# Two opening weight units taken through the input tiles together, their weights loaded in halves

## The chip, the cores and the metric

The program runs on one core of one Trainium2 chip. The metric is the device time of one execution in microseconds (us), lower is better. Each kernel is executed several times, and the median is compared.

## The reference, cut to what matters

The program computes a dilated attention block, a retention block and a stick-breaking attention block, each followed by a gated feed-forward layer, on 512 positions of width 1024 in float32. The change touches only the first normalisation and the first products of the first block:

```python
def rms_norm(x, g):
    xf = x.astype(jnp.float32)
    y = xf * lax.rsqrt(jnp.mean(xf * xf, axis=-1, keepdims=True) + EPS)
    return (y * g.astype(jnp.float32)).astype(x.dtype)
...
    h = rms_norm(x, ln_pre_mix[l])
    proj = h @ w_in[l]
    u_pool = proj[..., :POOL_WIDTH]
    q = proj[..., POOL_WIDTH:POOL_WIDTH + ATTN_WIDTH].reshape(B, S, N_HEADS, HEAD_DIM)
    k = proj[..., POOL_WIDTH + ATTN_WIDTH:POOL_WIDTH + 2 * ATTN_WIDTH].reshape(B, S, N_HEADS, HEAD_DIM)
    v = proj[..., POOL_WIDTH + 2 * ATTN_WIDTH:].reshape(B, S, N_HEADS, HEAD_DIM)
    q, k = rope(q, pos), rope(k, pos)
```

The 256 columns of `u_pool` are two blocks of 128 columns; each of the six head pairs then takes one block of q, one of k and one of v.

## The kernel before

**Units.** The input lies transposed in eight tiles of 128x512 (`X[:, c, :]`, c = 0 to 7). All weights come as a stream of units: a unit is a block of 1024 rows by 128 columns, 512 KB, in eight 128x128 pieces. To reach float32 precision, every input tile and every unit is split into a high part and a low part in a shorter format: HH and HL of the input, WH and WL of the weights. A unit is 24 matmul passes of 128x512 on TensorE (PE): for each of eight pieces WH with HH, WH with HL, and WL with HH. Units 0 and 1 are the two pooling blocks, unit 2 the q block, unit 3 the k block and unit 4 the v block of the first head pair.

**Who does what.** ScalarE (ACT) makes HH (`input_hi`, L1527) and WH (`split_hi`, L375, and two half copies at L1830 and L1833). VectorE (DVE) makes HL (`input_lo`, L2182). GpSimd (POOL) makes WL by a subtraction of a whole unit, 128x1024 (`split_lo`, L647), except for unit 0, which DVE makes in two halves of 128x512 (L2603, L2608). There are two sets of RAW, WH and WL: even units use set 0 and odd units set 1; unit 4 has a raw buffer of its own, RAW7, but uses WH and WL of set 0. The load of a unit into a raw buffer waits until the low part of the unit two before it is made (semaphore `s_lo`), because that subtraction reads the raw buffer.

**The queues.** The SyncE queue (SP) issues in program order: the gains, x tiles 1 and 2, the second half of unit 0, x tiles 5 and 7, the first half of unit 1, then unit 2 (which waits for the low part of unit 0), then seven constant tables (L589), then unit 4 (L592), unit 3 and unit 5 (L570). The ACT queue issues x tile 0, the first half of unit 0, x tiles 3, 4 and 6, and the second half of unit 1.

**TensorE's order.** Three products of zeros (L1149), then `first_unit` for unit 0, which goes tile by tile with its low part two tiles behind (L1138, L1141, L1142); then unit 1 whole (`use_unit`: `high_part`, L394 and L395, then `low_part`, L403); then the first attention stage, `attn_stage(0, None)`: the high part of unit 2, the mean of the squares (`mean_of_sum`, L714), the low part of unit 2, unit 3 whole, and unit 4. Before unit 4 PE waits until DVE has turned the q block (`a_qk`), because unit 4 writes the same PSUM bank as unit 2.

**The norm.** The inverse root of the mean is not applied to the input but to the results. ACT squares the eight tiles (L1837), DVE adds them up into ACC (`add_squares`, L2501 and L2504), PE takes the mean over partitions (L714), ACT forms the logarithm into ACC (L1536) and the exponential into RB (L1538). DVE multiplies the cosine and sine tables by RB (L2617, CS1 and SN1), multiplies the q block by the cosine table (L2660), ACT copies the halves of the q block crosswise (L1875), and DVE multiplies by the sine table and adds (L2664, L2668), which gives QT1. POOL's subtraction for unit 1 waits until all HL are made, and that for unit 2 and the following ones until all squares are added.

```python
                    pool.wait_ge(s_h, DC)
                    split_lo(Unit(1), chunks)

                    pool.wait_ge(s_sq_used, DC)
                    for n in range(2, 6):
                        split_lo(Unit(n), chunks)
```

On ACT the order after the eight HH is: WH of unit 1, eight squares, WH of unit 2, WH of unit 3, MEANR (L1841, a copy of a constant), the logarithm, the exponential, WH of unit 4, the four crosswise copies.

Of the kernel before, what the change touches and what calls it, by code (L numbers as in the profile page):

```python
# [135 lines left out]
def build(nc, ins, out_t):  # L136
    ctx = ExitStack()
    with ctx:
# [423 lines left out]
        def _(sp):  # L562
# [11 lines left out]
            for count, chunks, large in STRETCHES:  # L574
                stream = ins["w_large" if large else "w_small"].rearrange("u p (c n) -> u p c n", c=chunks)
                start = 0
                if first == 0:
# [4 lines left out]
                    sp.dma_start(RAW[0][:, 4:DC, :], stream[0][:, 4:DC, :]).then_inc(s_raw[0], 16)  # L582
                    for c in (5, 7):
                        sp.dma_start(X[:, c, :], ins["x_t"][:, c, :]).then_inc(s_x_in[c], 16)
                    sp.dma_start(RAW[1][:, 0:4, :], stream[1][:, 0:4, :]).then_inc(s_raw[1], 16)
# [4 lines left out]

                    sp.wait_ge(s_raw[0], Unit(2).m * 16 + 16)
                    sp.dma_start(RAW7[:], stream[4]).then_inc(s_raw[0], 16)  # L592
                    load_unit(Unit(3), stream[3], chunks)
# [46 lines left out]
        def _(pool):  # L640
# [19 lines left out]
            for count, chunks in stretches:  # L660
# [5 lines left out]
                if first == 0:  # L666

                    pool.wait_ge(s_h, DC)
                    split_lo(Unit(1), chunks)

                    pool.wait_ge(s_sq_used, DC)
                    for n in range(2, 6):
                        split_lo(Unit(n), chunks)
                    start = 3
# [34 lines left out]
        def _(pe):  # L709
# [420 lines left out]
            def first_unit(u, bank):  # L1130

                for c in range(DC + 2):
                    if c in (0, 4):
                        pe.wait_ge(*((s_first_hi, 1) if c == 0 else (s_hi, u.index + 1)))
                    if c in (2, 6):
                        pe.wait_ge(*((s_first_lo, 1) if c == 2 else (s_lo, u.index + 1)))
                    if c >= 2:
                        mm = pe.matmul(bank, WL[u.s][:, c - 2, :], HH[:, c - 2, :], start=False, stop=(c == DC + 1))  # L1138
                    if c < DC:
                        pe.wait_ge(s_h, c + 1)  # L1140
                        pe.matmul(bank, WH[u.s][:, c, :], HH[:, c, :], start=(c == 0), stop=False)  # L1141
                        hi = pe.matmul(bank, WH[u.s][:, c, :], HL[:, c, :], start=False, stop=False)  # L1142
                        if c == DC - 1:
                            hi.then_inc(s_hi_used, 1)
                mm.then_inc(s_unit, 1)
# [4 lines left out]
            first_unit(Unit(0), B[2][:])  # L1150
            use_unit(pe, Unit(1), B[3][:], DC, HH, HL)
# [365 lines left out]
        def _(act):  # L1517
# [646 lines left out]
        def _(dve):  # L2164
# [331 lines left out]
            def add_squares(n):  # L2496

                for c in range(1, DC):
# [3 lines left out]
                    else:  # L2502
                        dve.wait_ge(s_sq_used, 8 * n + c)
                        dve.tensor_tensor(ACC[:], ACC[:], SQ4[:, c, :], ALU.add).then_inc(s_sq_used, 1)  # L2504

# [91 lines left out]
            for c in range(DC):  # L2597
                dve.wait_ge(s_x_in[c], 16)
                input_lo(0, c, G_MIX1)
                if c == 1:  # L2600
                    dve.wait_ge(s_first, 16)
                    dve.wait_ge(s_first_hi, 1)
                    dve.tensor_tensor(WL[0][:, 0:4, :], RAW[0][:, 0:4, :], WH[0][:, 0:4, :].bitcast(F32),  # L2603
                                      ALU.subtract).then_inc(s_first_lo, 1)
                if c == 3:
                    dve.wait_ge(s_raw[0], 16)
                    dve.wait_ge(s_hi, 1)
# [533 lines left out]
```

## Time and profile before

| | |
|---|---|
| median of 3 runs | 1918.2 us (1917.78 to 1918.5) |
| the profiled execution's own time | 1917.92 us |
| its span in the trace | 1916.0 us |
| PE busy | 1908.2 us |
| DVE, ACT, POOL busy | 1146.5, 880.0, 466.8 us |
| granted TensorE clock | 1.000 |
| read from HBM | 174.30 MB |

The profiled execution's own time is 1.9 us above its span, which is what lies around the first and the last instruction. Matmuls overlap, so a busy time per matmul is longer than the distance between two starts; distances are read from the starts.

### The profile page before, as it was taken

How to read it: one execution, taken by the hardware profiler on the slowest of the kernel's cores; microseconds unless marked ns; L12 is line 12 of the kernel's file. 1: busy time of each engine (PE TensorE's matmuls, PEld its weight loads, DVE VectorE, ACT ScalarE, POOL GpSimd, SP SyncE). 2: the span in 40 equal slices, each digit the busy share in tenths (PEclk: the TensorE clock that was granted, in tenths of full speed). 3: DMA queues.
4: the chain of work that ended last, by engine and by line, in shares of the span. 5: the costliest groups of instructions: out<-in, count | busy, mean ns of one | idle time of the engine just before them, and what ended most of it. 6: DMA issues, size and time to landing. Idle time of an engine off the chain costs nothing.

```text
span 1916.0 us, 28674 instructions
## 1 busy us (share of the span) xinstructions
PE 1908.2 (100%) x10163; PEld 1614.7 (84%) x10163; DVE 1146.5 (60%) x1663; ACT 880.0 (46%) x1370; POOL 466.8 (24%) x181
## 2 busy tenths in 40 slices
PE   9999999999999999999999999999999999999999
PEld 6777889998888888888889998888777788999887
DVE  5775688866237455464267787423777768877500
ACT  6665544435234434434254444324667554444421
POOL 3323300003423343343420000443322240000243
PEclk9999999999999999999999999999999999999999
DMA  5222233223323222232333222232212133222332
GB/s 177 66 67 77 68 127 114 99 77 106 101 79 108 71 97 82 73 107 66 99 110 110 99 99 89 104 105 76 68 60 66 55 115 113 103 99 77 102 106 89
DMA packets 48892, 177.45 MB, mean 93 GB/s; under 512 B 5552, under 2 KB 6448, under 8 KB 48816
## 3 DMA queue, kind: packets, MB, share of 16 engines
q1 hardware_dynamic: 37440, 139.39, 22.2%
q10 hardware_dynamic: 11376, 37.03, 5.6%
q8 instruction: 50, 0.82, 0.2%
q14 instruction: 26, 0.21, 0.0%
HBM read 174.30 MB, written 2.10 MB: 92 GB/s over the span
## 4 chain that ended last, share of the span: by engine, by line
PE 98%; DVE 1%; DMA 0%; ACT 0%; issue 0%; SPq 0%; DVEq 0%; ACTq 0%
PE B L394 20%; PE B L395 20%; PE B L403 20%; PE B L870 6%; PE B L866 5%; PE B L868 5%; PE B L1217 1%; PE B L415 1%; PE B L1221 1%; PE B L1218 1%; PE B L420 1%; PE B L416 1%; PE B L1398 1%; PE B L1435 1%; PE B L1421 1%; PE B L1045 1%
## 5 line engine op out<-in xcount | busy, mean ns | idle before, releaser
L647 POOL TENSOR_TENSOR WL<-RAW,WH 128x1024 fp32r<-128x1024 f32 (+1 forms) x170 | 455.8, 2684 | 1423.8 <-ACT WH L375 858.2
L375 ACT CAST WH<-RAW 128x1024 fp32r<-128x1024 f32 (+1 forms) x236 | 262.4, 1114 | 454.2 <-PE B L395 365.5
L394 PE MATMUL B<-HH,WH 128*128 128x512 f32 x1096 | 431.0, 393 | 0.1
L395 PE MATMUL B<-HL,WH 128*128 128x512 f32 x1096 | 427.6, 390 | 0.0
L403 PE MATMUL B<-HH,WL 128*128 128x512 f32 x1096 | 272.9, 391 | 0.0
L394 PEld LDWEIGHTS B<-HH,WH 128*128 128x128 f32 x1096 | 205.8, 188 | 43.4 <-issue 1.7
L395 PEld LDWEIGHTS B<-HL,WH 128*128 128x128 f32 x1096 | 206.0, 188 | 41.2
L403 PEld LDWEIGHTS B<-HH,WL 128*128 128x128 f32 x1096 | 202.9, 188 | 41.5 <-POOL WL L647 0.4
L394 PE MATMUL B<-MH,WH 128*128 128x512 f32 x440 | 171.2, 389 | 0.0
L395 PE MATMUL B<-ML,WH 128*128 128x512 f32 x440 | 171.2, 389 | 0.0
L870 PE MATMUL B<-TH,SL 128*128 128x256 f32 x512 | 143.8, 281 | 0.0
L866 PE MATMUL B<-TH,SH 128*128 128x256 f32 x512 | 143.8, 281 | 0.0
L868 PE MATMUL B<-TL,SH 128*128 128x256 f32 x512 | 143.8, 281 | 0.0
L2454 DVE TENSOR_TENSOR X<-X,B 128x512 f32 x26 | 17.9, 687 | 203.2 <-PE B L403 193.3
L2177 DVE TENSOR_TENSOR ACC<-ACC,SQ 128x512 f32<-128x512 f32 x38 | 74.6, 1964 | 107.8 <-ACT SQ L1524 107.6
L1577 ACT CAST SH<-SUMS 128x512 fp32r<-128x512 f32 (+1 forms) x96 | 73.4, 765 | 125.9 <-DVE SUMS L2262 87.7
L866 PE MATMUL B<-HH,SH 128*128 128x256 f32 x384 | 107.8, 281 | 0.0
L870 PE MATMUL B<-HH,SL 128*128 128x256 f32 x384 | 107.8, 281 | 0.0
L868 PE MATMUL B<-HL,SH 128*128 128x256 f32 x384 | 107.8, 281 | 0.0
L403 PE MATMUL B<-MH,WL 128*128 128x512 f32 x429 | 103.6, 389 | 0.0
L868 PEld LDWEIGHTS B<-TL,SH 128*128 128x128 f32 x512 | 98.0, 191 | 2.4
L866 PEld LDWEIGHTS B<-TH,SH 128*128 128x128 f32 x512 | 96.1, 188 | 2.6
(429 smaller groups left out, 3581.7 us busy)
## 6 DMA issues: line engine op xcount, KB each, us to landing
RAW<-in_w_small SPq DMA_DIRECT2D x190, 512.0 KB, 3.5
RAW<-in_w_large SPq DMA_DIRECT2D x48, 704.0 KB, 4.1
SUMS<-in_w_seven ACTq DMA_DIRECT2D x32, 512.0 KB, 3.6
R<-in_w_seven ACTq DMA_DIRECT2D x17, 512.0 KB, 4.5
HD<-in_w_seven ACTq DMA_DIRECT2D x15, 512.0 KB, 4.5
out_t<-X SPq DMA_DIRECT2D x7, 256.0 KB, 5.2
X<-in_x_t ACTq DMA_DIRECT2D x4, 256.0 KB, 6.4
X<-in_x_t SPq DMA_DIRECT2D x4, 256.0 KB, 6.8
```

Source lines behind the costliest of these rows:

```text
L375: act.copy(wh, raw).then_inc(s_hi, 1)
L394: pe.matmul(bank, wh[:, c, :], xh[:, k0 + c, :], start=(start and c == 0), stop=False)
L395: mm = pe.matmul(bank, wh[:, c, :], xl[:, k0 + c, :], start=False, stop=False)
L403: mm = pe.matmul(bank, wl[:, c, :], xh[:, k0 + c, :], start=False, stop=(stop and c == chunks - 1))
L415: pe.matmul(bank, wh[:, c, :], xh[:, k0 + c, :], start=(start and c == 0), stop=False)
L416: pe.matmul(bank, wh[:, c, :], xl[:, k0 + c, :], start=False, stop=False)
L647: pool.tensor_tensor(wl, raw, wh.bitcast(F32), ALU.subtract).then_inc(s_lo, 1)
L866: pe.matmul(bank, wh, xh[:, rows.start + c, cols], start=(start and c == 0), stop=False, skip_group_check=True)
L868: pe.matmul(bank, wh, xl[:, rows.start + c, cols], start=False, stop=False, skip_group_check=True)
L870: mm = pe.matmul(bank, wl, xh[:, rows.start + c, cols], start=False, stop=(c == 3), skip_group_check=True)
L1577: act.copy(SH7[:, form, :], src).then_inc(t_hi, 1)
L2177: dve.tensor_tensor(ACC[:], ACC[:], SQ[b][:], ALU.add).then_inc(s_sq_used, 1)
```

## The change

Five edits, all in the opening.

1. Loads. The ACT queue now issues the first half of unit 1 (L1836 of the changed kernel) straight behind the first half of unit 0, ahead of x tiles 3, 4 and 6. The SP queue issues the second half of unit 1 behind the second half of unit 0, ahead of x tiles 5 and 7. Unit 3 is issued before unit 4, straight behind the constants.
2. ACT. WH of both units is made in halves among the HH: unit 0's first half behind tile 0, unit 1's behind tile 1, the second halves behind tiles 3 and 4. WH of unit 2 is made after the fifth of the eight squares.
3. DVE. It makes WL of units 0 and 1 in four halves: behind tiles 0 and 1, and behind tiles 4 and 5 (before: unit 0's behind tiles 1 and 3). It also makes WL of unit 2, by one 128x1024 subtraction between the adds of the squares.
4. POOL no longer makes WL of units 1 and 2; it starts with unit 3, still behind the last square.
5. PE. `first_two_units` replaces `first_unit` and `use_unit` for units 0 and 1: the same 48 passes, six for each tile.

```diff
                     sp.dma_start(RAW[0][:, 4:DC, :], stream[0][:, 4:DC, :]).then_inc(s_raw[0], 16)
+                    sp.dma_start(RAW[1][:, 4:DC, :], stream[1][:, 4:DC, :]).then_inc(s_raw[1], 16)
                     for c in (5, 7):
                         sp.dma_start(X[:, c, :], ins["x_t"][:, c, :]).then_inc(s_x_in[c], 16)
-                    sp.dma_start(RAW[1][:, 0:4, :], stream[1][:, 0:4, :]).then_inc(s_raw[1], 16)
                     load_unit(Unit(2), stream[2], chunks)
                     sp.wait_ge(s_x_in[DC - 2], 16)
                     for dst, name in CONSTS:
                         sp.dma_start(dst, ins[name]).then_inc(s_const, 16)
 
+                    load_unit(Unit(3), stream[3], chunks)
                     sp.wait_ge(s_raw[0], Unit(2).m * 16 + 16)
                     sp.dma_start(RAW7[:], stream[4]).then_inc(s_raw[0], 16)
-                    load_unit(Unit(3), stream[3], chunks)
...
-                    pool.wait_ge(s_h, DC)
-                    split_lo(Unit(1), chunks)
-
                     pool.wait_ge(s_sq_used, DC)
-                    for n in range(2, 6):
+                    for n in range(3, 6):
                         split_lo(Unit(n), chunks)
...
+                for step, u, c in ((hi_hi, 0, 0), (hi_lo, 0, 0), (hi_hi, 0, 1), (lo_hi, 0, 0), (hi_hi, 1, 0),
+                                   (hi_lo, 1, 0), (hi_lo, 0, 1), (lo_hi, 0, 1), (hi_hi, 1, 1), (hi_lo, 1, 1),
+                                   (lo_hi, 1, 0), (lo_hi, 1, 1)):
+                    step(u, c)
+                for c in range(2, 6):
+                    for step in (hi_hi, hi_lo, lo_hi):
+                        for u in range(2):
+                            step(u, c)
+                for u in range(2):
+                    for step in (hi_hi, hi_lo, lo_hi):
+                        for c in (6, 7):
+                            step(u, c)
...
             act.dma_start(RAW[0][:, 0:4, :], small[0][:, 0:4, :]).then_inc(s_first, 16)
+            act.dma_start(RAW[1][:, 0:4, :], small[1][:, 0:4, :]).then_inc(s_second, 16)
             for c in (3, 4, 6):
                 act.dma_start(X[:, c, :], ins["x_t"][:, c, :]).then_inc(s_x_in[c], 16)
-            act.dma_start(RAW[1][:, 4:DC, :], small[1][:, 4:DC, :]).then_inc(s_second, 16)
...
                 input_hi(c, G_MIX1)
-                if c == 1:
-                    act.wait_ge(s_first, 16)
-                    act.copy(WH[0][:, 0:4, :], RAW[0][:, 0:4, :]).then_inc(s_first_hi, 1)
-                if c == 3:
-                    act.wait_ge(s_raw[0], 16)
-                    act.copy(WH[0][:, 4:DC, :], RAW[0][:, 4:DC, :]).then_inc(s_hi, 1)
-            act.wait_ge(s_second, 16)
-            split_hi(act, Unit(1), DC)
+                if c < 2:
+                    act.wait_ge((s_first, s_second)[c], 16)
+                    act.copy(WH[c][:, 0:4, :], RAW[c][:, 0:4, :]).then_inc(s_first_hi, 1)
+                if c in (3, 4):
+                    act.wait_ge(s_raw[c - 3], 16)
+                    act.copy(WH[c - 3][:, 4:DC, :], RAW[c - 3][:, 4:DC, :]).then_inc(s_hi, 1)
             for c in range(DC):
                 act.activation(SQ4[:, c, :], X[:, c, :], ACT.Square).then_inc(s_squared, 1)
-            split_hi(act, Unit(2), DC)
+                if c == 4:
+                    split_hi(act, Unit(2), DC)
             split_hi(act, Unit(3), DC)
...
-            add_squares(0)
+            add_squares(0, {4: Unit(2)})
             rnorm(0)
```

VectorE's queue at the start, before the change. In these rows HL is the low part of an input tile, WL0 and WL1 are the low parts of even and odd units, ACC the sum of squares:

```order
L2182 SCALAR_TENSOR_TENSOR HL<-X,GAINS,HH 128x512 [waits input_hi,x_landed1]
L2603 TENSOR_TENSOR WL0<-RAW0,WH0 128x512 [waits first_half_weights_hi,first_half_weights_landed]
L2182 SCALAR_TENSOR_TENSOR HL<-X,GAINS,HH 128x512 [waits input_hi,x_landed2]
L2182 SCALAR_TENSOR_TENSOR HL<-X,GAINS,HH 128x512 [waits input_hi,x_landed3]
L2608 TENSOR_TENSOR WL0<-RAW0,WH0 128x512 [waits weights_hi,raw_landed0]
L2182 SCALAR_TENSOR_TENSOR HL<-X,GAINS,HH 128x512 [waits input_hi,x_landed4]
```

The same place in the changed kernel, down to the norm's tables:

```order
L2196 SCALAR_TENSOR_TENSOR HL<-X,GAINS,HH 128x512 [waits input_hi,x_landed4]
L2624 TENSOR_TENSOR WL0<-RAW0,WH0 128x512 [waits weights_hi,raw_landed0]
L2196 SCALAR_TENSOR_TENSOR HL<-X,GAINS,HH 128x512 [waits input_hi,x_landed5]
L2624 TENSOR_TENSOR WL1<-RAW1,WH1 128x512 [waits weights_hi,raw_landed1]
L2196 SCALAR_TENSOR_TENSOR HL<-X,GAINS,HH 128x512 [waits input_hi,x_landed6]
L2196 SCALAR_TENSOR_TENSOR HL<-X,GAINS,HH 128x512 [waits input_hi,x_landed7]
L2515 TENSOR_TENSOR ACC<-SQ4 128x512 [waits squared]
L2518 TENSOR_TENSOR ACC<-ACC,SQ4 128x512 [waits square_added,squared] x3
L2528 TENSOR_TENSOR WL0<-RAW0,WH0 128x1024 [waits weights_lo,unit_done,weights_hi]
L2518 TENSOR_TENSOR ACC<-ACC,SQ4 128x512 [waits square_added,squared] x3
```

The second half of unit 0's low part, which the load of unit 2 waits for, stood behind tile 3 and now stands behind tile 4.

SyncE's queue behind the x tiles, before the change. RAW0, RAW1 and RAW7 are the raw buffers, and `weights_lo` is the semaphore of the low parts:

```order
L570 DMA RAW0<-in_w_small 128x1024 [waits weights_lo]
L589 DMA IDENT<-in_ident 128x128 [waits x_landed6]
L589 DMA MEAN<-in_mean 128x128
L589 DMA BIAS<-in_bias 128x512
L589 DMA CS1<-in_cos1 128x512
L589 DMA SN1<-in_sin1 128x512
L589 DMA INV<-in_inv_counts 128x1024
L589 DMA WPOOL<-in_w_pool 128x256
L592 DMA RAW7<-in_w_small 128x1024 [waits raw_landed0]
L570 DMA RAW1<-in_w_small 128x1024 [waits weights_lo] x2
```

The same place in the changed kernel:

```order
L570 DMA RAW0<-in_w_small 128x1024 [waits weights_lo]
L589 DMA IDENT<-in_ident 128x128 [waits x_landed6]
L589 DMA MEAN<-in_mean 128x128
L589 DMA BIAS<-in_bias 128x512
L589 DMA CS1<-in_cos1 128x512
L589 DMA SN1<-in_sin1 128x512
L589 DMA INV<-in_inv_counts 128x1024
L589 DMA WPOOL<-in_w_pool 128x256
L570 DMA RAW1<-in_w_small 128x1024 [waits weights_lo]
L593 DMA RAW7<-in_w_small 128x1024 [waits raw_landed0]
```

Unit 3 (RAW1) and unit 4 (RAW7) have changed places; both still stand behind unit 2 and the seven constants.

## Rows read from the trace of the kernel before

**Rows 1.** The page, section 1: busy us, share and instructions of TensorE.

```profile
PE 1908.2 (100%) x10163; PEld 1614.7 (84%) x10163; DVE 1146.5 (60%) x1663; ACT 880.0 (46%) x1370; POOL 466.8 (24%) x181
```

**Rows 2.** Waits of PE, longest total: us in total, times, longest us.

```profile
PE B L1149 <- POOL RB L650: 1.3, 1, 1.3
```

**Rows 3.** Timeline of PE: start us, us, engine, line, operation, count.

```profile
6.89 0.50 PE L1141 MATMUL B<-HH,WH 128*128 128x512 f32 x1 [0.97 <-ACT WH L1830]
...
19.98 0.39 PE L394 MATMUL B<-HH,WH 128*128 128x512 f32 x1
...
23.62 1.02 PE L714 MATMUL B<-ACC,MEAN 128*128 128x512 f32 x2
...
26.32 0.39 PE L394 MATMUL B<-HH,WH 128*128 128x512 f32 x1
...
32.06 0.50 PE L394 MATMUL B<-HH,WH 128*128 128x512 f32 x1
```

**Rows 4.** Timeline of ACT, DVE and POOL around the norm, 22 to 28 us.

```profile
22.27 1.05 ACT L375 CAST WH<-RAW 128x1024 fp32r<-128x1024 f32 x1 [3.61 <-DMA RAW<-in_w_small]
...
23.22 0.29 ACT L1841 CAST MEANR<-MEAN 128x128 fp32r<-128x128 f32 x1
...
24.68 0.69 ACT L1536 ACTIVATE ACC<-B,GAINS 128x512 f32<-128x512 f32 x1 [1.16 <-PE B L714]
...
25.94 1.04 ACT L375 CAST WH<-RAW 128x1024 fp32r<-128x1024 f32 x1
26.07 0.74 DVE L2617 TENSOR_TENSOR CS<-CS,RB 128x512 f32<-128x512 f32 x1 [4.63 <-ACT RB L1538]
...
26.73 0.68 DVE L2617 TENSOR_TENSOR SN<-SN,RB 128x512 f32<-128x512 f32 x1
...
27.05 2.62 POOL L647 TENSOR_TENSOR WL<-RAW,WH 128x1024 fp32r<-128x1024 f32 x1 [0.79 <-ACT WH L375]
```

**Rows 5.** Timeline of DVE and ACT in the opening, 9 to 22 us.

```profile
9.65 0.69 DVE L2608 TENSOR_TENSOR WL<-RAW,WH 128x512 fp32r<-128x512 f32 x1
...
10.49 2.04 ACT L1527 ACTIVATE HH<-X,GAINS 128x512 fp32r<-128x512 f32 x3 [0.41 <-DMA X<-in_x_t]
...
11.32 2.08 DVE L2182 SCALAR_TENSOR_TENSOR HL<-X,GAINS,HH 128x512 fp32r<-128x512 f32 x3 [0.32 <-ACT HH L1527]
...
16.75 4.68 DVE L2504 TENSOR_TENSOR ACC<-ACC,SQ 128x512 f32<-128x512 f32 x6
```

**Rows 6.** Timeline of the DMA queues: issue of x tile 6, unit 2 and unit 4.

```profile
2.64 0.66 ACTq L1822 DMA_DIRECT2D X<-in_x_t  x1
...
10.37 0.33 SPq L570 DMA_DIRECT2D RAW<-in_w_small  x1
...
14.06 0.71 SPq L592 DMA_DIRECT2D RAW<-in_w_small  x1
```

**Rows 7.** DMA view at those issues and WPOOL's: count, KB, us from issue to landing.

```profile
X<-in_x_t ACTq DMA_DIRECT2D x1, 256.0 KB, 8.0
...
RAW<-in_w_small SPq DMA_DIRECT2D x1, 512.0 KB, 3.5
...
RAW<-in_w_small SPq DMA_DIRECT2D x1, 512.0 KB, 6.9
WPOOL<-in_w_pool SPq DMA_DIRECT2D x1, 128.0 KB, 6.2
```

**Rows 8.** Timeline of POOL and DVE, 177 to 184 us, the second norm.

```profile
177.68 2.41 POOL L647 TENSOR_TENSOR WL<-RAW,WH 128x1024 fp32r<-128x1024 f32 x1 [17.62 <-ACT WH L375]
178.15 2.49 DVE L2177 TENSOR_TENSOR ACC<-ACC,SQ 128x512 f32<-128x512 f32 x1 [2.54 <-ACT SQ L1524]
...
180.05 2.84 POOL L647 TENSOR_TENSOR WL<-RAW,WH 128x1024 fp32r<-128x1024 f32 x1
180.77 2.67 DVE L2177 TENSOR_TENSOR ACC<-ACC,SQ 128x512 f32<-128x512 f32 x1
```

**Rows 9.** Stretches: us, busy us of PE, PEld, DVE, ACT, POOL, granted clock, DMA share, GB/s.

```profile
1.00:6.00 5.00, 4.61 (x6) 1.71 (x6) 0.53 (x1) 2.39 (x3) 2.14 (x4) 1.00 0.79 248
```

More of the change, by code:

```diff
@@ L1127, in attn_stage, with first_two_units, hi_hi, hi_lo @@
                         pool_product(POOL_ENDS[a])
-            def first_unit(u, bank):
-                for c in range(DC + 2):
+            def first_two_units():
+                def hi_hi(u, c):
                     if c in (0, 4):
[L1134 to L1139, printed above, removed]
-                        pe.wait_ge(s_h, c + 1)
[L1141 to L1145, printed above, removed]
+                        pe.wait_ge(*((s_first_hi, u + 1) if c == 0 else (s_hi, u + 1)))
+                    if u == 0:
+                        pe.wait_ge(s_h_hi, c + 1)
+                    pe.matmul(B[2 + u][:], WH[u][:, c, :], HH[:, c, :], start=(c == 0), stop=False)
+                def hi_lo(u, c):
+                    if u == 0:
+                        pe.wait_ge(s_h, c + 1)
+                    mm = pe.matmul(B[2 + u][:], WH[u][:, c, :], HL[:, c, :], start=False, stop=False)
+                    if c == DC - 1:
+                        mm.then_inc(s_hi_used, 1)
+                def lo_hi(u, c):
+                    if c in (0, 4):
+                        pe.wait_ge(*((s_first_lo, u + 1) if c == 0 else (s_lo, u + 1)))
+                    mm = pe.matmul(B[2 + u][:], WL[u][:, c, :], HH[:, c, :], start=False, stop=(c == DC - 1))
+                    if c == DC - 1:
+                        mm.then_inc(s_unit, 1)
+                for step, u, c in ((hi_hi, 0, 0), (hi_lo, 0, 0), (hi_hi, 0, 1), (lo_hi, 0, 0), (hi_hi, 1, 0),
[10 more added lines that the diff above has]
+                            step(u, c)
@@ L1149, in _ @@
                 pe.matmul(B[7][:], RB[:, 0:P], RB[:], start=True, stop=True)
-            first_unit(Unit(0), B[2][:])
-            use_unit(pe, Unit(1), B[3][:], DC, HH, HL)
+            first_two_units()
             attn_stage(0, None)
@@ L2494, in sum_lo, with add_squares @@
                 dve.tensor_tensor(ACCL[:], ACC[:], ACCH[:].bitcast(F32), ALU.subtract).then_inc(s_sum_lo, 1)
-            def add_squares(n):
+            def add_squares(n, lows={}):
                 for c in range(1, DC):
@@ L2504, in add_squares @@
                         dve.tensor_tensor(ACC[:], ACC[:], SQ4[:, c, :], ALU.add).then_inc(s_sq_used, 1)
+                    if c in lows:
+                        weights_lo(lows[c])
             def weights_lo(u):
@@ L2599, in _ @@
                 input_lo(0, c, G_MIX1)
[L2600 to L2603, printed above, removed]
+                if c < 2:
+                    dve.wait_ge((s_first, s_second)[c], 16)
+                    dve.wait_ge(s_first_hi, c + 1)
+                    dve.tensor_tensor(WL[c][:, 0:4, :], RAW[c][:, 0:4, :], WH[c][:, 0:4, :].bitcast(F32),
                                       ALU.subtract).then_inc(s_first_lo, 1)
-                if c == 3:
-                    dve.wait_ge(s_raw[0], 16)
-                    dve.wait_ge(s_hi, 1)
-                    dve.tensor_tensor(WL[0][:, 4:DC, :], RAW[0][:, 4:DC, :], WH[0][:, 4:DC, :].bitcast(F32),
-                                      ALU.subtract).then_inc(s_lo, 1)
-            add_squares(0)
+                if c in (4, 5):
+                    dve.wait_ge(s_raw[c - 4], 16)
+                    dve.wait_ge(s_hi, c - 3)
+                    dve.tensor_tensor(WL[c - 4][:, 4:DC, :], RAW[c - 4][:, 4:DC, :],
+                                      WH[c - 4][:, 4:DC, :].bitcast(F32), ALU.subtract).then_inc(s_lo, 1)
+            add_squares(0, {4: Unit(2)})
             rnorm(0)
```

## The prediction

> **What bounds the kernel now.** I read the page first: TensorE is busy for 1908.2 us of a span of 1916.0 [rows 1], so a change wins only what PE idles, and loses whatever new idle it makes. The waits of PE say that no single wait is longer than 1.3 us [rows 2]. The timeline of PE gives the stages of the opening [rows 3]: the first useful pass starts at 6.89, unit 2 at 19.98, the mean of the squares at 23.62, unit 3 at 26.32, unit 4 at 32.06. From 19.98 to 23.62 there are 16 passes, 0.2275 us each. Two places idle. Units 0 and 1 are 48 passes, 10.92 us, and take 19.98 - 6.89 = 13.09: 2.17 us of waiting for input tiles. Unit 3 is 24 passes, 5.46, and so ends at 31.78, while unit 4 starts at 32.06: 0.28 us of waiting for the turned q block.
>
> That second wait is the one to follow, because everything behind unit 4 is PE work in a fixed order: the program ends as much earlier or later as unit 4 starts. The reader should see the chain to it in the timeline of the other engines [rows 4]: ACT makes WH of unit 3 at 22.27, as soon as its load has landed, then MEANR at 23.22, the logarithm at 24.68, the exponential, WH of unit 4 at 25.94; DVE multiplies the two tables at 26.07 and 26.73, done at 27.41; the rest of the q block takes 32.06 - 27.41 = 4.65 us up to unit 4. POOL's subtraction for unit 4 begins at 27.05.
>
> **The change, part by part.**
>
> *The 48 passes.* Their number stays. With six passes a tile PE has more to do per landed tile, so it waits less. 2.17 us is the ceiling, and up to 0.4 more for an earlier first pass, since WH of unit 0 now stands behind one HH, not two (an HH is 2.04/3 = 0.68 [rows 5]). Against it, half of unit 1 is now loaded ahead of tiles 3, 4 and 6, one place later on their queue. I take unit 2 to start at 18.7, 1.3 us earlier.
>
> *The load of unit 2, and all behind it.* On DVE the second half of WL0 ended at 9.65 + 0.69 = 10.34 [rows 5] and SP issued unit 2 at 10.37 [rows 6]. Now that half stands behind HL of tile 4. Tile 4 is now the fifth entry of the ACT queue. The entry in that place before was issued at 2.64 [rows 6] and landed 8.0 later [rows 7], at 10.64; sizes and places of the queue are as before, so tile 4 lands there. HH starts then, HL 11.32 - 10.49 = 0.83 later, HL takes 2.08/3 = 0.69 and WL0's half 0.69 [rows 5]: done at 12.9. So unit 2 is issued at 12.95, 2.6 us later than now, and with it the seven constants and units 3 and 4, which stand behind it on SP. Unit 2 itself lands 3.5 later [rows 7], at 16.5, in time for 18.7.
>
> *The load of unit 3.* It now has the place that unit 4 had, 14.06 - 10.37 = 3.69 behind unit 2 [rows 6], and landed 6.9 after its issue [rows 7]. That gives 12.95 + 3.69 + 6.9 = 23.5. Before, unit 3 landed at 22.2 (ACT's wait ends at 22.27 [rows 4]). Moving it ahead of unit 4 thus doesn't make up for the later start of the queue. Bounds: 3.5 after its issue, as unit 2 had, would be 20.1; I take the row of the same place in the same queue.
>
> *Squares and mean.* WL of unit 2 goes from POOL to DVE: twice a half of 0.69, so 1.4 us, between adds of 4.68/6 = 0.78 [rows 5]. Two further halves of 0.69 stand among the HL. From WL0's half at 12.9, two HL, the other half and the last HL follow back to back, four times 0.69, if the last x tile is there by 14 (before, its HH began by 10.49 + 2 x 0.68 = 11.85, and it moves back one place): HL are done at 15.7, four adds at 18.8, WL of unit 2 at 20.2, the last three adds at 22.5. The constants, which PE waits for ahead of the mean, end with WPOOL: 6.2 after an issue [rows 7] that is one of eight places, 3.69/8 = 0.46, ahead of unit 3's 16.64, so at 22.4. PE itself has done the high part at 18.7 + 3.6 = 22.3. The mean starts at 22.5, 1.1 earlier than 23.62. If nothing else came in, unit 4 would start 1.1 earlier.
>
> *The norm on ACT.* The logarithm stands behind WH of unit 3 and MEANR. From the start of WH of unit 3 to the end of MEANR is 23.22 + 0.29 - 22.27 = 1.24 [rows 4], so it can't start before 23.5 + 1.3 = 24.8, whatever the mean does. That is 0.1 later than the 24.68 of before: the mean's 1.1 us are gone at this point.
>
> *POOL against VectorE.* Before, the tables met no long operation of POOL and took 0.74 and 0.68 [rows 4]. Now POOL's first subtraction is unit 3's. It starts when WH of unit 3 is made: 23.5 + 1.05 + 0.15 = 24.7, and takes 2.4, to 27.1. DVE asks for the cosine table at 24.8 + 26.07 - 24.68 = 26.2. Two operations with both inputs in SBUF don't run side by side here: in the second norm an add of this size that takes 0.78 elsewhere took 2.49, from 178.15 to 0.55 behind the end of POOL's 177.68 + 2.41 [rows 8]. The rule of the Trainium skill (SBUF — State Buffer, "SBUF: two separate sides") is that the two engines share a port pair as an exclusive lock for the whole instruction; by that rule, the trace agrees. So the cosine table ends at 27.1 + 0.55 = 27.65. Meanwhile ACT has made WH of unit 4 (24.8 + 1.26 + 1.04 = 27.1 by the distances of rows 4), and POOL asks for its next subtraction at 27.2, ahead of that 27.65. Who is next? The same stretch shows it: POOL's second began at 180.05, waited for the add to end at 180.64, then ran 2.4 while DVE's second add, asked for at 180.77, took 2.67 [rows 8]. They alternate. So POOL runs from 27.65 to 30.0 and the sine table ends at 30.0 + 0.55 = 30.6, against 27.41 before. Behind it 4.65 us as before: unit 4 starts at 35.25.
>
> **Sum.** 35.25 - 32.06 = +3.2 us. PE reaches the mean 1.1 earlier and idles some 4.6 us ahead of unit 4, instead of 0.28. Nothing behind unit 4 can take it back, since PE has no idle there. Against the profiled execution's own 1917.9 that is 1921.1; the median of the runs stands 0.3 above that execution, so I forecast 1921.4. A measurement of this kernel can hardly tell less than 0.2%, 3.8 us, from no change; the forecast lies just inside.
>
> **The rivals.**
>
> *A: the early load, a gain.* If unit 3 lands by 21.8, POOL's subtraction of it is over and the cosine table done before POOL asks for unit 4; ACT's logarithm then follows the mean, at 23.6, and unit 4 starts at about 31.0, -1.1 us: 1917.1. With tiles landing as early as now it would be up to -2.2, 1916.0. For it: the 6.9 us of unit 4's load had x tiles and unit 1 on both queues not long before. Against it: unit 2, issued into just that backlog, landed in 3.5. The Trainium skill (DMA: Bandwidth & Descriptors, "Anatomy of one DMA") fits one load from GpSimd's queue by 2.0 us plus bytes at 436 GB/s, 3.2 us for 512 KB; by it unit 3 would land at 19.8 and this rival hold. Rows 7 have double that behind the constants.
>
> *B: delay without the second block.* If DVE keeps its turn after the cosine table, the sine table ends at 28.3, and unit 4 starts at 33.0, +0.9; if the two never meet, only the later logarithm counts, +0.1. 1918.3 to 1919.1.
>
> *C: TensorE's clock falls, clearly slower.* The forecast has PE idle for 4.6 us, more than three times its longest wait of now. All slices grant 2.4 GHz. Yet the six records of products of zeros in the opening are 4.61 us long [rows 9], 0.77 each, against 1.02/2 = 0.51 for the same kind at 23.62 [rows 3]: PE starts slow after standing still. If the same 4.61 us come again behind unit 4's wait, they cost 4.61 x (1 - 0.51/0.77) = 1.6 us, to +4.8: 1923.0. It decides once the idle is long enough; 1.3 is not. The Trainium skill (TensorE: Matmul & The Clock Gate, Part 1) says the clock of an idle array is halved and activity restores it; no row shows a fall in the middle of this kernel.
>
> **How the numbers follow.** Forecast 0.45: three rows carry it, and each step has half a microsecond of room. A 0.25, B 0.15, C 0.13, and 0.02 for something larger on the good side. The load time of unit 3 moves the forecast one for one; with 0.6 either way its own range is 1920.8 to 1922.2. The range of 8 in 10 runs from 1917.0 (A's likely value) to 1922.6; it leaves out C and A's lower end. Slower by over 0.2%: all of C and a tenth of the forecast's case, 0.17. Faster by over 0.2% would need more than PE idles in the whole opening: 0.02. Within: 0.81.
>
> **What would show it.** In the changed profile: unit 2 issued near 13.0 and landed near 16.5; the mean at 22.5; WH of unit 3 at 23.5; the cosine table 1.4 us long or more and the sine table about 3 us, with POOL's operation between them; unit 4's first pass near 35.2, with a PE wait of over 4 us put down to QT. WH of unit 3 before 22, or both table operations at 0.7, refute the forecast in favour of A. A wait as forecast but passes 0.4 us apart behind it are C.

## The result, and the profile after

The changed kernel takes 1924.64 us, the median of 7 runs (1922.39 to 1925.44), against 1918.01 for the kernel before (7 runs, 1917.78 to 1918.50). The ratio is 1.0029, with a 95% interval of 1.0020 to 1.0038: slower, by 6.6 us between the medians and by 5.6 us by the ratio. The forecast was 1921.4, range 1917.0 to 1922.6. The profiled execution took 1922.39 us with a span of 1920.4, 4.4 above the span of before; the other executions are slower than the profiled one, and both parts have to be explained.

The page, section 1, against [rows 1]:

```profile
PE 1910.4 (99%) x10163; PEld 1617.6 (84%) x10163; DVE 1150.7 (60%) x1666; ACT 880.0 (46%) x1371; POOL 462.0 (24%) x179
```

PE's waits (us in total, times, longest us), against [rows 2]:

```profile
PE B L394 <- DVE QT L2684: 4.3, 1, 4.3
PE B L1165 <- POOL RB L650: 1.3, 1, 1.3
```

The timeline of PE, against [rows 3]: the first useful pass, unit 2, the mean, unit 3, unit 4 and two of its passes further on.

```profile
6.56 0.80 PE L1134 MATMUL B<-HH,WH 128*128 128x512 f32 x1
...
18.60 0.39 PE L394 MATMUL B<-HH,WH 128*128 128x512 f32 x1
...
22.23 1.02 PE L711 MATMUL B<-ACC,MEAN 128*128 128x512 f32 x2
...
24.94 0.39 PE L394 MATMUL B<-HH,WH 128*128 128x512 f32 x1
...
34.80 0.80 PE L394 MATMUL B<-HH,WH 128*128 128x512 f32 x1 [4.25 <-DVE QT L2684]
35.38 0.63 PE L395 MATMUL B<-HL,WH 128*128 128x512 f32 x1
...
38.27 0.39 PE L394 MATMUL B<-HH,WH 128*128 128x512 f32 x1
```

Unit 2 starts 1.4 us earlier than before, the mean 1.4, unit 3 1.4: the opening does what the change says. Then PE waits 4.25 us, and unit 4 starts 2.74 us later than before. That is not all: the eight passes from 34.80 to 38.27 take 3.47 us, 0.43 apart, where the same eight took 1.96 before, from 32.06 [rows 3] to this one:

```profile
34.02 0.40 PE L394 MATMUL B<-HH,WH 128*128 128x512 f32 x1
```

The timeline of ACT, DVE and POOL around the norm, against [rows 4]:

```profile
23.20 1.05 ACT L375 CAST WH<-RAW 128x1024 fp32r<-128x1024 f32 x1 [3.54 <-DMA RAW<-in_w_small]
24.16 0.29 ACT L1855 CAST MEANR<-MEAN 128x128 fp32r<-128x128 f32 x1
24.36 0.68 ACT L1551 ACTIVATE ACC<-B,GAINS 128x512 f32<-128x512 f32 x1
24.39 2.41 POOL L647 TENSOR_TENSOR WL<-RAW,WH 128x1024 fp32r<-128x1024 f32 x1 [21.25 <-ACT WH L375]
25.73 1.62 DVE L2633 TENSOR_TENSOR CS<-CS,RB 128x512 f32<-128x512 f32 x1 [4.09 <-ACT RB L1553]
26.75 2.86 POOL L647 TENSOR_TENSOR WL<-RAW,WH 128x1024 fp32r<-128x1024 f32 x1
27.27 2.88 DVE L2633 TENSOR_TENSOR SN<-SN,RB 128x512 f32<-128x512 f32 x1
```

ACT waits for unit 3's load and starts the logarithm right behind MEANR, though the mean was ready earlier. Then POOL and DVE take turns: the cosine table ends 0.55 behind POOL's first subtraction (24.39 + 2.41 = 26.80, and 27.35), POOL's second, begun at 26.75, runs until 29.61, and the sine table ends 0.54 behind that, at 30.15. The two tables took 0.74 and 0.68 before.

The issue of units 2 and 3 on SP, and what each took to land, against [rows 6, 7]:

```profile
12.75 0.33 SPq L570 DMA_DIRECT2D RAW<-in_w_small  x1
...
16.44 0.58 SPq L570 DMA_DIRECT2D RAW<-in_w_small  x1
```

```profile
RAW<-in_w_small SPq DMA_DIRECT2D x1, 512.0 KB, 3.4
...
RAW<-in_w_small SPq DMA_DIRECT2D x1, 512.0 KB, 6.7
```

The stretches behind the wait (us, busy us of PE, PEld, DVE, ACT, POOL, granted clock, DMA share, GB/s), first of the changed kernel and then of the kernel before:

```profile
35.00:38.00 3.00, 3.00 (x8) 2.35 (x9) 1.75 (x4) 2.31 (x4) 1.98 (x1) 0.50 0.00 0
38.00:44.00 6.00, 6.00 (x30) 4.59 (x30) 2.30 (x4) 1.05 (x1) 1.83 (x1) 0.99 0.31 87
```

```profile
35.00:38.00 3.00, 3.00 (x15) 2.26 (x15) 1.53 (x3) 1.27 (x2) 0.10 (x1) 1.00 0.52 175
38.00:44.00 6.00, 6.00 (x35) 4.82 (x34) 4.34 (x19) 2.82 (x9) 2.26 (x1) 1.00 0.27 89
```

A granted clock of 0.50 is the lower of the two levels, 1.2 GHz: 8 matmuls in 3 us instead of 15. So the profiled execution loses 2.74 us to the late start and 1.51 to the clock, 4.25 of its 4.4.

### The profile page after: what moved, and what is told of

It reads as the page before. It is cut to its first block, busy times and chain, and to the rows that moved or that the text cites. A ratio compares the mean times of both kernels' runs of the same rounds, so it can differ in the third digit from the quotient of the medians.

```text
span 1920.4 us, 28677 instructions
## 1 busy us (share of the span) xinstructions
PE 1910.4 (99%) x10163; PEld 1617.6 (84%) x10163; DVE 1150.7 (60%) x1666; ACT 880.0 (46%) x1371; POOL 462.0 (24%) x179
## 3 DMA queue, kind: packets, MB, share of 16 engines
q1 hardware_dynamic: 37440, 139.39, 22.5%
## 4 chain that ended last, share of the span: by engine, by line
PE 97%; DVE 1%; DMA 1%; issue 0%; ACT 0%; SPq 0%; ACTq 0%; DVEq 0%
PE B L394 20%; PE B L395 20%; PE B L403 20%; PE B L867 6%; PE B L863 5%; PE B L865 5%; PE B L1232 1%; PE B L415 1%; PE B L1236 1%; PE B L1233 1%; PE B L420 1%; PE B L416 1%; PE B L1413 1%; PE B L1450 1%; PE B L1436 1%; PE B L1042 1%
## 5 line engine op out<-in xcount | busy, mean ns | idle before, releaser
L647 POOL TENSOR_TENSOR WL<-RAW,WH 128x1024 fp32r<-128x1024 f32 (+1 forms) x168 | 451.0, 2688 | 1433.1 <-ACT WH L375 873.4
```

The source lines that it names most:

```text
L647: pool.tensor_tensor(wl, raw, wh.bitcast(F32), ALU.subtract).then_inc(s_lo, 1)
```

## The experiments

Three statements are to be told from their rivals. First, unit 4 is late because the load of unit 3 is late, and because GpSimd's subtractions and VectorE's tables take turns. Second, the clock falls because of the idle and nothing else. Third, what makes the other executions slower than the profiled one. The kernels were run in four groups, each with runs of the kernel before beside it, and each is compared with those of its own group.

**Idle alone, first try.** Memsets on VectorE behind the sine table of the kernel before, four in one kernel and eight in the other:

```diff
             for tab in (CS1, SN1):
                 steps.done(dve.tensor_tensor(tab[:], tab[:], RB[:], ALU.mult))
+            for k in range(4):
+                dve.memset(PT[:, 0, 0:T], 0.0).then_inc(IDLE, 1)
+                dve.wait_ge(IDLE, k + 1)
```

> The kernel before, with four memsets of 128x512 on VectorE behind the sine table, so that the q block, and with it unit 4, comes about 2.2 us later. Theory (the clock falls when TensorE idles long enough ahead of unit 4): an idle of about 2.4 us is too short, the time grows by the 2.2 us and no more, about 1920.2. Rival (the passes behind the wait are slow for another reason, such as the half-loaded weights): also +2.2. If any idle lowers the clock: +4 or more.

> The same with eight memsets, about 4.4 us, so that TensorE idles about 4.7 us ahead of unit 4 as in the changed kernel, with nothing else of the change. Theory: the clock falls and the time grows by 4.4 plus 1.7 to 4 us, 1924 to 1926, with passes 0.43 us apart behind the wait and run times spread over some us. Rival (slow passes come from the change's new order): +4.4 only, 1922.4, passes at 0.23.

Measured: 1922.06 (1919.79 to 1926.02, 11 runs) and 1925.71 (1924.76 to 1929.71, 5 runs) against 1918.34. The second is as the theory has it: PE waits 5.4 us, the granted clock is 0.57 from 36 to 40 us, and the span grows by 6.8. The first did not test what it was made for. In its profiled execution GpSimd came between the two tables, in a kernel that has nothing of the change:

```profile
25.11 1.11 DVE L2617 TENSOR_TENSOR CS<-CS,RB 128x512 f32<-128x512 f32 x1 [4.27 <-ACT RB L1538]
...
26.10 2.39 POOL L647 TENSOR_TENSOR WL<-RAW,WH 128x1024 fp32r<-128x1024 f32 x1 [0.42 <-ACT WH L375]
26.15 2.89 DVE L2617 TENSOR_TENSOR SN<-SN,RB 128x512 f32<-128x512 f32 x1
```

The logarithm was one us earlier there (23.72, not 24.68), GpSimd's subtraction of unit 3 ended behind the request of the cosine table, and the sine table again took 2.89 us; PE waited 5.2 us where 2.4 were meant. So the kernel before is itself near this order. It also means that the first experiment can't say what 2 us of idle do.

**The wait filled with work.** Eighteen products whose result is not used, in PE's wait ahead of unit 4:

```diff
+                    if first:
+                        pe.wait_ge(s_mean_r, 1)
+                        for _ in range(18):
+                            pe.matmul(B[6][:], MEANR[:], HH[:, 0, :], start=True, stop=True)
                     pe.wait_ge(a_qk, j * 2 + 1)
                     high_part(pe, u + 2, B[0][:], DC, HH, HL)
```

> The changed kernel, with 18 products (MEANR with an input tile, result unused) that TensorE runs in the wait ahead of unit 4, 4.1 us in all. Theory: unit 4 starts at 34.8 as before but its passes run at 0.23 from the first one, so the time is that of the late start alone, before + 2.7, about 1920.8, with little spread. Rival (the loss of 6.6 us is more than the wait and the clock, something later in the program also loses): 1922 or more with passes at 0.23 in unit 4.

Measured: 1923.71 (1922.69 to 1928.08, 5 runs) against 1918.34, not the 1920.8 of the theory: by the times the rival came true, something later loses as well. The profile does show what was meant: unit 4 starts at 35.25, PE waits 0.2 us instead of 4.25, and the granted clock is 1.00 in every stretch. By the starts of the same passes in the two traces, this execution is 3.2 us behind the kernel before at 36 us, all late start, and 4.7 behind at the end; 1.25 of the rest are lost at one place around 1 ms, at which no other variant loses anything:

```profile
PE B L863 <- ACT SQ L1664: 1.0, 1, 1.0
...
1017.65 6.11 DMA HD<-in_w_seven
```

The first line is PE's wait there, the second the load to which the chain of work behind it goes back: issued at 1017.65, it landed 6.1 us later. In the first profile of the changed kernel VectorE's add behind the same load began 4.6 us after its issue (1018.69, 1023.28), here 6.2 us. So that loss is a late landing; why it was late isn't known. Three of the five executions show a mean clock below 1.000. The filler takes the clock's part away at unit 4 in the profile. The run times don't show it: even the two executions at 1.000 took 1922.7 and 1923.4.

**GpSimd behind the tables.**

```diff
                     for n in range(3, 6):
+                        if n == 4:
+                            pool.wait_ge(s_dve, 2)
                         split_lo(Unit(n), chunks)
```

> The changed kernel, with GpSimd's subtraction for unit 4 waiting until VectorE has made both tables. Theory (they alternate on what they share): the cosine table still takes about 1.6 us, the sine table 0.7 instead of 2.9, unit 4 starts some 2.3 us earlier, near 32.6, with an idle of 2 us and no slow passes: before + 0.5, about 1918.5. Rival (VectorE waits for something else there, such as the root): no change against the changed kernel, 1924.6.

Measured: 1920.79 (1918.90 to 1921.63, 11 runs) against 1918.34, 2.0 us more than expected. The turns are as the theory has them: the cosine table still takes 1.61, behind the subtraction for unit 3, and the sine table 0.68 instead of 2.88.

```profile
25.54 1.61 DVE L2635 TENSOR_TENSOR CS<-CS,RB 128x512 f32<-128x512 f32 x1 [4.16 <-ACT RB L1555]
...
27.07 0.68 DVE L2635 TENSOR_TENSOR SN<-SN,RB 128x512 f32<-128x512 f32 x1
```

Unit 4 starts at 32.40, near the 32.6 expected. What was not expected is behind it:

```profile
PE B L394 <- DVE QT L2686: 2.2, 1, 2.2
```

```profile
32.00:36.00 4.00, 3.60 (x10) 2.83 (x11) 2.65 (x5) 2.31 (x4) 2.54 (x1) 0.67 0.32 126
```

Behind an idle of 2.2 us the clock fell. Eight of the eleven executions show a mean granted clock of 0.999, three 1.000.

**The low part of unit 3 on VectorE.**

```diff
-            add_squares(0, {4: Unit(2)})
+            add_squares(0, {4: Unit(2), 7: Unit(3)})
...
-                    for n in range(3, 6):
+                    pool.wait_ge(s_lo, 4)
+                    for n in range(4, 6):
                         split_lo(Unit(n), chunks)
```

> The changed kernel, but VectorE also makes the low part of unit 3, behind the last square, and GpSimd starts with unit 4. Theory (the two tables lost 2.4 us to GpSimd's subtractions of units 3 and 4): the tables take 0.7 each, unit 4 starts near 31.7 with 1.3 us of idle, no fall of the clock; 0.3 us below the kernel before, about 1917.8, with little spread. Rival (the late load of unit 3 alone makes the loss): unit 4 still at 34 or later, 1922 or more.

Measured: 1919.03 (1918.22 to 1919.99, 11 runs) against 1918.14. Both tables take 0.69 us and the spread is small: the turns are gone. Unit 4 starts at 32.96, not 31.7, since unit 2 was issued at 13.25 and unit 3 landed at 24.48 in the profiled execution. PE idles 1.3 us there without a fall; three of eleven executions show 0.999, and how long PE idled in those is not known. The forecast of 1917.8 is missed by 1.2 us.

**Four constants ahead of unit 2 on SP, alone and with the edit above.**

```diff
-                    load_unit(Unit(2), stream[2], chunks)
                     sp.wait_ge(s_x_in[DC - 2], 16)
-                    for dst, name in CONSTS:
+                    for k, (dst, name) in enumerate(CONSTS):
+                        if k == 4:
+                            load_unit(Unit(2), stream[2], chunks)
                         sp.dma_start(dst, ins[name]).then_inc(s_const, 16)
```

> The changed kernel, but SyncE issues four of the seven constants ahead of unit 2, in the time in which it waits for the low part of unit 0 (11.0 to 12.8). Theory (unit 3 lands 1 us late because the whole queue behind unit 2 is late): unit 3 is issued near 14.7 and lands near 21.4, the logarithm follows the mean at 23.3, and unit 4 starts near 31, if GpSimd's subtraction of unit 3 (22.6 to 25.0) is over in time: 1916.9 to 1918, in some executions 2 to 4 us more, since the order of the two engines is decided by a tenth of a us. Rival (the place in the queue doesn't set the landing): unit 3 at 23 again, 1924.

> Both edits together. Theory: no late load and no collision; unit 4 starts when TensorE comes to it, at 30.5 to 30.8, with less than 0.4 us of idle; 1.3 to 1.5 us below the kernel before, about 1916.9, little spread: the gain that the change's new order of the passes holds. Rival: as the kernel before or slower, which would mean that the wait ahead of unit 4 has another cause.

Measured: 1919.22 (1918.09 to 1922.48) and 1919.25 (1918.29 to 1922.94), 11 runs each, against 1918.14. Both miss. Tile 6, which the constants wait for, landed only at about 12.2 in the profiled execution of the first (the first constant is issued at 12.18), so unit 2 was issued at 13.97 and its load took 5 us behind the constants. WH of unit 2 came at 19.14, and PE waited for it, 1.2 us, at the start of unit 2. The edit moved the wait from unit 4 to unit 2. In the second, PE waited 1.0 us at that place and 1.8 us for the first half of unit 1 in the opening, with the granted clock at 1.00 throughout.

**The changed kernel once more.**

> The changed kernel once more, for a second profile and on the same chip as the others. Expected: unit 4 starts at 34.8 give or take 0.3 again, the sine table takes about 2.9 us; the time 1922.5 to 1925.5, since the stretch of slow passes behind the idle varies from run to run. If the slow passes number more than 8 here and the time is higher by 0.2 us for each, the spread of the run times is the clock's.

Measured: 1923.81 (1922.89 to 1924.62, 7 runs) against 1918.14. Unit 4 starts at 36.24, not at 34.8 give or take 0.3, and this profile shows what the first one doesn't:

```profile
PE B L394 <- DVE QT L2684: 3.3, 1, 3.3
PE B L1134 <- ACT WH L1845: 1.4, 2, 1.2
```

```profile
9.00:13.00 4.00, 3.75 (x10) 2.94 (x10) 2.94 (x5) 3.69 (x7) 0.00 (x0) 0.57 0.62 239
...
36.00:40.00 4.00, 3.76 (x10) 2.96 (x11) 2.64 (x5) 2.31 (x4) 2.42 (x1) 0.59 0.09 12
```

The clock falls twice, once already in the opening. The order of the 48 passes has PE wait for the first half of unit 1 after four passes. Here that half landed 6.9 us after its issue, at 8.6; ACT converted it at 8.58, in the first profile at 7.83. PE idled 1.2 us instead of 0.4, and ran at the lower level from 9.4 to 12.9 us. The mean starts at 24.59 instead of 22.23, unit 4 at 36.24 instead of 34.80, and the span is 1921.8, 1.4 above that of the first profile.

The fall in the opening is not what makes unit 4 late. The late loads are:

```profile
13.56 0.33 SPq L570 DMA_DIRECT2D RAW<-in_w_small  x1
...
24.65 1.05 ACT L375 CAST WH<-RAW 128x1024 fp32r<-128x1024 f32 x1 [2.63 <-DMA RAW<-in_w_small]
...
25.80 0.68 ACT L1551 ACTIVATE ACC<-B,GAINS 128x512 f32<-128x512 f32 x1
```

Tile 4's HH begins at 11.36, not 10.54, so unit 2 is issued 0.81 later (13.56 against 12.75), and unit 3, issued 0.82 later, takes 7.4 us to land, not 6.7. WH of unit 3 is 1.45 later and the logarithm, behind it and MEANR, 1.44: all that unit 4 is late by. The mean alone, with the 1.06 us that lay between the mean and the logarithm before, would have let the logarithm start at 25.65. What the opening lost stayed inside PE's wait ahead of unit 4, which shrank from 4.25 to 3.3.

Six of these seven executions have a mean clock of 0.998, and the profile with two falls is one of them; the profiles with one fall show 0.999. The first comparison has four executions at 0.999, two at 0.998, one at 0.997.

**Work in the opening's wait.** Four products, result not used, ahead of unit 1's first pass:

```diff
+                    if step is hi_hi and (u, c) == (1, 0):
+                        for _ in range(4):
+                            pe.matmul(B[6][:], WH[0][:, 0, :], HH[:, 0, :], start=True, stop=True)
                     step(u, c)
```

> The changed kernel, with four products (unit 0's first piece with tile 0, result unused) in TensorE's wait ahead of unit 1's first pass, 0.9 us. Theory (in the executions in which the first half of unit 1 lands late, the clock falls already in the opening and costs 1.5 us once more): the slow executions go, the median falls by 0.5 to 1 us against the changed kernel, to about 1923 to 1923.5, with a profile that shows full clock from 6 to 20. Rival (the spread is of the second wait alone): as the changed kernel, 1924.2.

Measured: 1923.95 (1922.48 to 1924.37, 7 runs). Full clock from 6 to 20 us in the profile, but three of seven executions still at 0.998, as many as stood at 0.998 or 0.997 in the first comparison, where six of seven did in the second: too few runs to say that the early fall goes. Against 1918.16 the median is where the changed kernel's was, and the 0.5 to 1 us that the theory has it drop by did not come. That fits the reading above, by which a fall in the opening costs the program nothing as long as the load of unit 3 is later still.

**Unit 2 in a raw buffer of its own.** RAW7 is free at that time; unit 4 then takes RAW0. Unit 2 no longer waits for the low part of unit 0, and the queue behind it neither:

```diff
-            if isinstance(u.m, int) and u.index == 4:
+            if isinstance(u.m, int) and u.index == 2:
                 return RAW7[:], WH[0][:, 0:DC, :], WL[0][:, 0:DC, :]
...
-                    load_unit(Unit(2), stream[2], chunks)
+                    sp.dma_start(RAW7[:], stream[2]).then_inc(s_third, 16)
...
-                    sp.dma_start(RAW7[:], stream[4]).then_inc(s_raw[0], 16)
+                    sp.dma_start(RAW[0][:, 0:DC, :], stream[4]).then_inc(s_raw[0], 16)
...
                 if c == 4:
+                    act.wait_ge(s_third, 16)
+                    act.sem_inc(s_raw[0], 16)
                     split_hi(act, Unit(2), DC)
```

> The changed kernel, but unit 2 is loaded into the raw buffer of its own (RAW7) and unit 4 into RAW0, so that SyncE issues unit 2 at 4.6 straight behind the x tiles and the constants at 11, without waiting for the low part of unit 0. Theory (the late queue behind unit 2 makes unit 3 late): constants landed by 21, unit 3 issued at 14.5 and landed near 21, mean at 22.3, logarithm at 23.4, unit 4 of TensorE at 30.8 to 31.5: 0.5 to 1.2 us below the kernel before, 1917.0 to 1917.6, with now and then the block of GpSimd. Rival (the x tiles are slowed by unit 2 behind them, or the gain is lost in the opening by a fall of the clock): 1918 to 1920.

> The same, and VectorE also makes the low part of unit 3. Theory: as before without the now and then: 1917.0 to 1917.4, the smallest spread of the changed variants; both tables 0.7 us. If it stays at 1918 or above with both tables at 0.7 and the constants early, the new order of the first 48 passes holds no gain on the chip.

Measured: 1917.38 (1916.71 to 1921.35) and 1917.95 (1916.94 to 1920.49), 11 runs each, against 1918.16. The ratios are 0.9998 (0.9989 to 1.0007) and 1.0000 (0.9991 to 1.0009): neither can be told from the kernel before, while the changed kernel's 1.0030 (1.0019 to 1.0042) can. The profile of the first:

```profile
21.30 1.06 ACT L376 CAST WH<-RAW 128x1024 fp32r<-128x1024 f32 x1 [1.24 <-DMA RAW<-in_w_small]
...
22.50 2.38 POOL L648 TENSOR_TENSOR WL<-RAW,WH 128x1024 fp32r<-128x1024 f32 x1 [19.36 <-ACT WH L376]
...
23.68 0.69 ACT L1552 ACTIVATE ACC<-B,GAINS 128x512 f32<-128x512 f32 x1 [1.12 <-PE B L712]
...
25.07 0.69 DVE L2636 TENSOR_TENSOR CS<-CS,RB 128x512 f32<-128x512 f32 x1 [3.03 <-ACT RB L1554]
25.68 0.69 DVE L2636 TENSOR_TENSOR SN<-SN,RB 128x512 f32<-128x512 f32 x1
...
31.01 0.50 PE L395 MATMUL B<-HH,WH 128*128 128x512 f32 x1
```

Unit 3 is issued at 15.58, 0.86 earlier than in the changed kernel's first profile and not at the 14.5 expected (tile 6, which the constants wait for, landed at about 12.3), and takes 5.7 us, not 6.7: it lands at 21.3. The logarithm now waits for the mean and not for the load, GpSimd is done with unit 3 before the tables, and unit 4 starts at 31.01, 1.05 us earlier than before. The one edit removes the late start, the turns and the idle together, in the profile; one of the eleven executions took 1921.35, at a mean clock of 0.999. The second kernel misses its forecast, 1917.0 to 1917.4 with the smallest spread: both tables take 0.7 us and unit 4 starts at 30.90, but two executions show 0.999, and the median is no better.

**The kernel before, with GpSimd behind the tables.** The two lines of the third experiment, in the kernel before.

> The kernel before, with GpSimd's subtraction for unit 4 waiting until both tables are made. Theory (the kernel before sits 0.3 us from the same block, and its few executions of 1920 and more are those in which GpSimd comes between the two tables): the same median, 1918.1, without the outliers above 1919.5. Rival: the outliers stay, or the wait costs something: 1918.5 or more.

Measured: 1918.30 (1917.58 to 1918.88, 11 runs) against 1918.16 (1917.18 to 1921.87, 29 runs, of which four above 1919). The median is as expected, and no execution is above 1919. With four such in 29, eleven executions would show none about one time in five, so that the wait removes them is not shown.

**Idle alone, clean.** The same kernel with three memsets:

> The kernel before, with GpSimd's subtraction for unit 4 held back until both tables are made (so that it can't come between them) and three memsets on VectorE, 2.0 us, behind the sine table: nothing of the change, one known idle of about 2.2 us ahead of unit 4. Theory (the clock falls in part of the executions at such an idle, whatever makes it): +2.0 us in the executions with granted clock 1.000 (1920.1) and +3.7 in the others (1921.8), a median between; tables at 0.7. Rival (2 us of idle are harmless, the change's load order or its halves of the weights made the slow passes): all executions near 1920.1.

Measured: 1920.25 (1919.33 to 1921.72, 11 runs) against 1918.00. The tables take 0.79 and 0.68, PE waits 2.0 us, and the profiled execution has a fall:

```profile
32.00:36.00 4.00, 2.42 (x6) 1.94 (x7) 3.27 (x5) 2.72 (x5) 2.55 (x1) 0.71 0.16 67
```

The seven executions with a mean clock of 1.000 took 1919.3 to 1920.3, the four with 0.999 took 1920.7 to 1921.7. The medians of the two groups lie 1.4 us apart. The idle alone lowers the clock, in part of the executions, without any of the change's edits; the same kernel without the memsets, above, has all eleven executions at 1.000. Of the 21 runs of the kernel before beside it, three took 1921.7 to 1922.0, all three at 0.999, and no other exceeded 1918.8. That looks like the same event, but none of the three was profiled.

**Both causes away.** The own raw buffer, and GpSimd behind the tables:

> The changed kernel with both causes taken away: unit 2 in its own raw buffer, and GpSimd's subtraction for unit 4 behind both tables. Theory: as the early load alone, 1917.4, with its executions above 1919 gone or fewer, 0.7 below the kernel before. Rival (the new order of the passes holds no gain): 1918.1 or more.

Measured: 1917.40 (1916.82 to 1918.62, 11 runs) against 1918.00; the ratio is 0.9993 with an interval of 0.9984 to 1.0002. No execution above 1918.7. It is the best version found, 0.6 us below the kernel before between medians, which these runs can't tell from no change.

## Why the prediction was wrong

Its direction and its first mechanism hold, step by step. Each pair is forecast and measured in the first profile: unit 2 issued 12.95 and 12.75; unit 2 landed 16.5 and 16.2; unit 3 landed 23.5 and 23.1; mean 22.5 and 22.23; logarithm 24.8 and 24.36; cosine table done 27.65 and 27.35; sine table done 30.6 and 30.15; unit 4 at 35.25 and 34.80. The late start came out as +2.74 where +3.2 stood: unit 2 was issued 0.2 us earlier, unit 3's load took 0.1 less, and the second turn 0.15 less. That last part could be read from [rows 8]: the prediction has GpSimd's second subtraction run 2.4 us behind the end of the add, but 180.05 + 2.84 - 180.64 is 2.25, and here it was 29.61 - 27.35 = 2.26. That the two engines alternate was right, and so, nearly, was the price of each turn. The forecast's own range, 0.6 either way, ends at 1922.0, not 1922.2.

Rival A, the early load, fell in the changed kernel: unit 3 took 6.7 us to land in this place of the queue, not 3.4. It did come true when unit 2 was taken out of the wait. Rival B fell with the second turn, 2.88 us for the sine table.

**The step that failed** is that the sum has no term for the clock. It has PE idle for 4.6 us ahead of unit 4 and lets every pass behind that run at full speed; the fall stands only in rival C, at 0.13. In the first profile the fall costs 1.51 us on top of the 2.74, and the text left open how long is long enough, with 1.3 us as the only row. Both profiles of the changed kernel have a fall at unit 4, and no execution of its two comparisons shows a mean clock of 1.000. Idle without anything of the change lowered it too: in all five executions of the kernel whose profile has 5.4 us of it, and in four of eleven of the one whose profile has 2.0 us. The likeliest case should have been the late start with the fall. Its value would have been C's, 1923.0, which is 0.6 above the profiled execution and 1.6 below the median.

C's mechanism was right, but its price of 1.6 was luck. It took 4.61 us with a third of it lost, from records of products of zeros over which the granted clock reads 1.00 [rows 9]. Measured are 3.47 us, of which 1.51, over two fifths, are lost at a granted clock of 0.50. The two errors cancel.

**What no case held** is the further 2.2 us between the profiled execution and the median. The second profile of the changed kernel accounts for 1.4 of it, by the mechanism of the forecast itself: x tile 4 landed 0.8 us later, unit 2 was issued as much later, and unit 3's load took 7.4 us, not 6.7. The prediction took landing times from one execution as fixed. It also gave the new order of passes no risk of its own, though it makes PE wait for a half unit after four passes; there the clock fell too, but that did not reach unit 4.

**Left open.** Whether filling the opening's wait removes the early fall; why loads land later in some executions; and the last 0.8 us between the second profile and the median of the first comparison.

## What to carry to other kernels

Reordering the first work to save a wait is worth only what the next join lets through: here 1.4 us of earlier passes met a load that the same reordering had made late, because the queue behind it waited for a step that had moved. Before moving a step, ask which queue waits for it and what stands behind it in that queue; a free buffer that removes the wait took the changed kernel from 5.7 us above the kernel before (1923.81 against 1918.14) to level with it (1917.38 against 1918.16, which the runs can't tell from no change). And count an idle of two us on TensorE as more than its length: here the passes behind it ran at half speed in some executions, and that cost 1.4 us more.

## What the runs showed of the hardware

- The clock of TensorE fell from 2.4 to 1.2 GHz (granted 0.50) in every profile with an idle of 2.0 us or more ahead of unit 4 (2.0, 2.2, 3.3, 4.2, 4.25, 5.2 and 5.4 us), and held in the one with 1.3 us there. Eight passes or so then ran 0.43 us apart, for a loss of some 1.5 us. In the opening the length of the idle alone doesn't tell: the clock fell after 1.2 us in the second profile of the changed kernel, and held after 1.8 us in the kernel with the constants first and VectorE making the low part of unit 3. Nor does it tell from one execution to the next: with 2.0 us added in the clean test, four of eleven show a fall. The Trainium skill (TensorE: Matmul & The Clock Gate, "HAM oscillation") says that gaps in TensorE's work lower its clock; the trace agrees, with the idles just named. It has longer gaps in mind than the shortest of these, and there the runs decide.
- Two operations that exclude each other also take turns: the engine that waits gets the next turn, so that a pair of 0.7 us operations behind a pair of 2.4 us ones took 1.62 and 2.88. The Trainium skill (SBUF — State Buffer, "SBUF: two separate sides") says that one of the two holds the shared ports for its whole instruction and the other blocks; the trace agrees, with 1.62 and 2.88 us. The order of the turns is what these rows show. Which pair comes first can hang on a us: in one execution of the kernel before with memsets added, the logarithm was 1.0 us earlier than before, and the tables took 1.11 and 2.89.
- The same DMA in the same place of the queue landed 6.1 us after its issue in one execution of the changed kernel (the first half of unit 1, converted at 7.83) and 6.9 in another (converted at 8.58), and unit 3's load 6.7 and 7.4.
